# Dealing the row steps of a PEER layer evenly over the late weight units, and making the residual in pieces

## What is computed

```
s1, s2 = q[:, :, 0] @ sub_keys_1.T, q[:, :, 1] @ sub_keys_2.T      # 8 heads, 128 keys each
top 16 of each, top 16 of their sums -> experts (n, 8, 16), gate = softmax(sums)
u   = u_table[experts]                  # 128 rows of 2048 floats for each token
act = gelu(einsum('nhkd,nd->nhk', u, x))
v   = v_table[experts]
out = einsum('nhk,nhkd->nd', gate * act, v)
y   = layer_norm(alpha * x + out)
```

## Time and profile before

| | |
|---|---|
| three runs | 4706.78, 4710.53, 4716.7 us |
| median | 4710.53 us |
| profiled execution | 4703.39 us, its span 4701.6 us |
| mean granted clock of TensorE | 0.965 |
| busy share | PE 92%, DVE 57%, ACT 23%, POOL 55% |
| bytes moved | 1081.84 MB |

### The profile page before, as it was taken

One profiled execution on the slowest core, in us unless ns is written; L12 is line 12 of the kernel. 1 busy time (PEld: TensorE's weight loads), 2 busy tenths in 40 slices (PEclk: granted clock), 3 DMA queues, 4 the chain that ended last, 5 costly groups with the idle time before them and its releaser, 6 DMA issues.

```text
span 4701.6 us, 74886 instructions
## 1 busy us (share of the span) xinstructions
PE 4333.9 (92%) x26508; PEld 4161.2 (89%) x26508; DVE 2686.9 (57%) x4819; ACT 1065.4 (23%) x1872; POOL 2598.3 (55%) x1718
## 2 busy tenths in 40 slices
PE   8999999999989997986877888799999999999996
PEld 8999888888889996985776878799999999999995
DVE  1000233344432315997996777777777777777777
ACT  1000122222221102001221222223332333333223
POOL 4454322222235452442326766688787888888883
PEclk9999999999999999997998988899999999999998
DMA  5222322321243221211448998899999999999995
GB/s 200 96 96 103 113 105 105 125 74 72 82 142 122 95 95 47 69 56 61 171 157 325 381 366 344 329 391 385 390 393 377 385 393 390 390 384 394 392 391 219
DMA packets 265955, 1081.84 MB, mean 230 GB/s; under 512 B 24496, under 2 KB 89136, under 8 KB 181168
## 3 DMA queue, kind: packets, MB, share of 16 engines
q0 software_dynamic: 74736, 544.24, 28.4%
q1 hardware_dynamic: 87840, 388.01, 22.6%
q10 hardware_dynamic: 103328, 148.96, 9.3%
HBM read 1019.65 MB, written 66.85 MB: 231 GB/s over the span
## 4 chain that ended last, share of the span: by engine, by line
PE 49%; issue 21%; DVE 11%; POOL 11%; DMA 6%; ACT 1%; POOLq 0%; DVEq 0%; ACTq 0%
PE banks L464 29%; PE banks L642 6%; PE banks L706 5%; POOL w_lo L329 5%; POOL work L365 4%; DMA work<-in_u_rows,idx 3%; PE banks L533 2%; PE banks L495 1%; PE banks L694 1%; POOL rows_own L365 1%; PE banks L503 1%; DVE work L1390 1%; DVE work L1303 1%; DVE work L1311 1%; DVE mv_hi L1389 1%
## 5 line engine op out<-in xcount | busy, mean ns | idle before, releaser
L329 POOL TENSOR_TENSOR w_lo<-w_raw,w_hi 128x1024 fp32r<-128x1024 f32 x480 | 1159.4, 2416 | 421.5 <-ACT w_hi L1027 418.4
L335 POOL TENSOR_SCALAR w_hi<-w_raw 128x2048 fp32r<-128x2048 f32 x130 | 254.0, 1954 | 1480.2 <-PE banks L464 1268.8
L464 PE MATMUL banks<-mv_hi,w_hi 128*128 128x256 f32 x3648 | 863.9, 318 | 62.7 <-DVE mv_lo L1137 37.2
L464 PE MATMUL banks<-mv_lo,w_hi 128*128 128x256 f32 x3648 | 836.6, 311 | 0.0
L464 PE MATMUL banks<-mv_hi,w_lo 128*128 128x256 f32 x3648 | 835.3, 310 | 0.0
L706 PE MATMUL banks<-mv_hi,w_hi 128*128 128x384 f32 x2048 | 704.4, 344 | 103.8 <-DVE work L1442 79.5
L464 PEld LDWEIGHTS banks<-mv_hi,w_hi 128*128 128x128 f32 x3648 | 652.2, 189 | 127.2 <-issue 102.3
L1027 ACT ACTIVATE w_hi<-w_raw 128x1024 fp32r<-128x1024 f32 x480 | 507.1, 1059 | 1065.3 <-PE banks L706 779.4
L642 PE MATMUL banks<-mv_hi,w_hi 128*128 128x384 f32 x2048 | 701.3, 342 | 44.5 <-POOL w_lo L329 28.6
L706 PE MATMUL banks<-mv_lo,w_hi 128*128 128x384 f32 x2048 | 699.0, 341 | 0.0
L706 PE MATMUL banks<-mv_hi,w_lo 128*128 128x384 f32 x2048 | 697.9, 341 | 0.0
(11 more groups left out here) (159 smaller groups left out, 4821.3 us busy)
## 6 DMA issues: line engine op xcount, KB each, us to landing
w_raw<-in_wstream SPq DMA_DIRECT2D x480, 512.0 KB, 8.1
w_raw<-in_wstream SPq DMA_DIRECT2D x130, 1024.0 KB, 4.8
gate_matrix<-work ACTq DMA_DIRECT2D x12, 2048.0 KB, 6.3
work<-gate_matrix ACTq DMA_DIRECT2D x32, 768.0 KB, 13.1
out_p<-work ACTq DMA_DIRECT2D x34, 320.0 KB, 2.2
work<-out_p ACTq DMA_DIRECT2D x34, 320.0 KB, 3.5
gate_scratch<-work ACTq DMA_DIRECT2D x32, 320.0 KB, 2.2
work<-gate_scratch ACTq DMA_DIRECT2D x16, 640.0 KB, 3.9
```

The costliest lines, as they stand in the source:

```text
L329: pool.tensor_tensor(w_lo[s][:, part], raw[s][:, part], w_hi[s][:, part].bitcast(f32), ALU.subtract) \
L335: pool.tensor_scalar(w_hi[s][:, :], raw[s][:, :], 1.0, 0.0, ALU.mult, ALU.add).then_inc(hi_done, 1)
L464: last = pe.matmul(acc(dst, h), a[s][:, P * k:P * k + P], b[h][:, k, :], start=(k == k_first and n == 0), stop=(k == k_last and n == 2))
```

## The change

The row steps get one list for all 240 late units. `deal()` gives each unit a room (7 for an activation unit, 6 for an output unit, 6, 5, 5.5, 4.5 for those of a mixed trip that also handle the early activations, 2 less in the first four, 0 in the last three) and a cost to each step (2, and 12 for the change of blocks), and deals them in order, so that `STEPS[k]` holds the numbers of unit k's steps. That makes 22, 25, 25 and 25 steps in the mixed trips, 17 or 18 in most groups (18, 18, 18, 17, 18, 18, 18, 17, 17 in groups 8 to 16, 14 in group 17, again 17 or 18 up to group 30, 12 in group 31). Passes no longer begin with a group: A on V begins in group 9, the blocks change in the first unit of group 17, B on V begins in group 24. The end of block B comes two units before the last.

```
+def deal():
+    steps = [[] for _ in ROOM]
...
+    scale = sum(ROOM) / sum(c for _, c in todo)
+    done, slot, room = 0, 0, ROOM[0]
+    for n, c in todo:
+        while room < (done + c / 2) * scale:
+            slot += 1
+            room += ROOM[slot]
+        steps[slot].append(n)
+        done += c
...
-MIXED = [3, 3, 3, 3, 4, 2, 2, 1, 3, 3, 3, 2]
-LATE_STEPS = [[2 * n, 2 * n + 1] for n in range(2 * EG)]
```

GpSimd, VectorE and ScalarE have these units written out instead of looped. The indices are read from `idx_all` directly, without the copy to `idx2` (L354), and the dots go straight to `act_n`, without `dots` and its copy. On GpSimd:

```
+            def position(k):
+                first = (len(STEPS[k]) + 1) // 2
+                for h, part in enumerate((STEPS[k][:first], STEPS[k][first:])):
+                    if k + 2 < len(STEPS):
+                        low(k % 2, k // 2 + 1, h)
+                    for n in part:
+                        if n == STEP_NORM:
+                            norm_store(0)
+                            for z in (0, 2, 3):
+                                gather(STEP_B_U + z)
+                            pool.wait_ge(n_stored, 16)
+                            gather(STEP_B_U + 1)
+                        else:
+                            fetch(n + ROWS)
 
             pool.wait_ge(idx_ready, 1)
-            fetch_idx(0, 0)
+            for n in range(ROWS - 1):
+                gather(n)
+            with pool.Fori((U_PEER + TAIL) // 2 + 1, U_LATE // 2) as i:
+                for s in range(2):
+                    split_next(s, i)
             for s in range(2):
                 for h in range(2):
                     low(s, 0, h)
...
+            for w in range(2):
+                pool.wait_ge(g_stored[w], 16 + 16 * (GBLK // 2))
+            gather(ROWS - 1)
```

```
             dve.wait_ge(picks_taken, 3)
+            dve.wait_ge(hb_stored, 16)
             dve.wait_ge(nat_ready, 2)
+            dve.sem_inc(rows_used, ROWS)
...
-            own.done(dve.tensor_scalar(r_acc, mv_hi[1].bitcast(f32), ALPHA, None, ALU.mult))
-            own.wait()
-            own.done(dve.scalar_tensor_tensor(r_acc, mv_lo[1].bitcast(f32), ALPHA, r_acc, ALU.mult, ALU.add))
...
+            def acc_low(e):
+
+                at = slice(EG * e, EG * e + EG)
+                dve.wait_ge(acc_high, e + 1)
+                own.done(dve.scalar_tensor_tensor(r_acc[:, at, :], mv_lo[1][:, at, :].bitcast(f32), ALPHA, r_acc[:, at, :],
+                                                  ALU.mult, ALU.add))
```

ScalarE serves the two gelus of the weights and the square roots of the norms at the unit where their step lies:

```
+            def serve(k):
+
+                for n in STEPS[k]:
+                    if n == STEP_A_V or n == STEP_B_V:
+                        act.wait_ge(act_n_ready, 1 if n == STEP_A_V else 2)
+                        act_n_gelu_pass()
+                    if n == STEP_NORM:
+                        act.wait_ge(n_var, 1)
+                        act.activation(rstd_n, rstd_n, ACT.Sqrt).then_inc(n_std, 1)
+                if k == STEPS_LAST + 1:
+                    act.wait_ge(n_var, 2)
+                    act.activation(rstd_n, rstd_n, ACT.Sqrt).then_inc(n_std, 1)
```

More of the change, by code:

```diff
@@ L383, in block_b @@
                 pool.dma_start(rows_t[2], hb_s).then_inc(rows_in[2], 16)
[L385 to L400, removed]
@@ L403, in position @@
[L403 to L415, removed]
@@ L417, in late_group, with fetch @@
[L417 to L422 removed]
+            def fetch(n):
+                if n in (STEP_NORM, STEP_NORM + 1):
+                    norm_row(n - STEP_NORM, STEP_NORM)
+                elif n == STEP_NORM + 2:
+                    block_b()
+                elif n in (STEP_END, STEP_END + 1):
+                    norm_row(n - STEP_END, STEP_END)
+                elif n < STEP_END and n != STEP_NORM + 3:
+                    gather(n)
@@ new lines, in steps @@
+            def steps(k, lo=0, hi=None):
+                for n in STEPS[k][lo:hi]:
+                    if n == STEP_NORM:
+                        block_change()
+                        continue
+                    if n == STEP_A_V or n == STEP_B_V:
+                        weights(n // PICKS // 2, n)
+                    gather_step(n)
+                if k == STEPS_LAST + 1 and lo == 0:
+                    norm_stats(1, STEP_END)
+                    norm_out(1, STEP_END)
+            def acc_low(e):
[3 more added lines that the diff above has]
+                                                  ALU.mult, ALU.add))
@@ new lines, in act_units @@
+            def act_units(g, q, k):
+                for e in range(EG):
+                    bank = banks[:, e, 0:N2]
+                    if e == 0:
+                        steps(k)
+                        dve.wait_ge(g4_in, 16 * q + 16)
+                    dve.wait_ge(gelu_done, 4 * g + e + 1)
+                    product(bank, e)
+                    if e < EG - 1:
+                        steps(k + e + 1, 0, 1)
+                    low_part(q, e, 0, bank)
+                    if k < EG:
+                        acc_low(e)
+                    if e < EG - 1:
+                        steps(k + e + 1, 1)
@@ L1567 @@
+            for g in range(2 * EARLY, GROUPS):
+                first, k = U_PEER + 8 * g + EG, U_PEER + 8 * g - U_LATE
+                act_units(g, g, k)
+                for v in range(EG):
+                    steps(k + EG + v, 0, 1 if v else None)
+                    add_out(g, v, first, g == GROUPS - 1, range(2))
+                    if v:
+                        steps(k + EG + v, 1)
+                    add_out(g, v, first, g == GROUPS - 1, range(2, 4))
+            layer_norm(1)
 def kernel(**inputs):
```

313 lines of the change are left out of this document (123 added, 190 removed).

## The result

The changed kernel took 4660.7 us (median of four, 4646.8 to 4672.0) where the kernel before took 4713.1 beside it: a ratio of 0.9893, 95% interval 0.9876 to 0.9911. The direction was right, but the gain is 52 us and not 106: the time lies at the end of the outer range (4555 to 4665) and outside the 4580 to 4635 of the forecast itself.

| piece | before | after | difference | forecast |
|---|---|---|---|---|
| up to the fourth gelu | 2521.2 | 2502.4 | -18.8 | -13 |
| four mixed trips | 546.3 | 448.5 | -97.8 | -115 |
| 23 late groups | 1546.4 | 1611.3 | +64.9 | +22 |
| what follows | 87.7 | 82.9 | -4.8 | 0 |

What follows compares the result with a forecast made beforehand. It took late groups to be bound by TensorE and mixed trips by DMA, with a 421 GB/s ceiling. Terms of -115, +22 and -13 summed to -106 us, giving 4604, between 4580 and 4635, outer range 4555 to 4665.

Steps and rivals of the forecast that it cites:

- What bounds the kernel: Kernel before: late groups bound by TensorE; mixed trips short of DMA by 17 us each, losing 37.
- (1) Trips: Four mixed trips: fewer row steps end the DMA shortage, leaving 107.8 us a trip; -115 us, bounds -135 and -75.
- (2) Groups: Late groups: 17 or 18 steps leave fifteen groups 0.94 us short of DMA; 24 us lost, bounds 0 and 60.
- The shortage sits in the first half: First half of a late group: 10 steps and 4 units need 34.9 us of DMA against 33.3.
- (3) The block change: Block change inside one late unit: 12 us lost where 14.9 were lost before, bounds 5 and 20.
- (4) Head: First four late units: early gathers and a residual in pieces shorten 61.5 us to 48.5; -13, bounds -5 and -18.
- (5) Tail: End of the kernel: second block's statistics delay additions by some 8 us; 0 taken, bounds -4 and +6.
- (6) loops: Written-out loops of VectorE, ScalarE and GpSimd: some 100 more code fetches cost 0, bounds -3 and +10.
- (a): DMA has room above 421 GB/s, so late groups lose nothing more: -147 us, 4563; chance 0.16.
- (b): Mixed trips keep half their loss because gate loads and early activations empty the DMA: 4658; chance 0.20.
- (c): Late groups: row queue crowds out weights, VectorE late at output units, 7.4 us lost in each: 4738; chance 0.07.

Runs made afterwards that it cites:

- Experiment 4: Changed kernel with four buffers for a mixed trip's early activations, all loaded at its start, instead of two used twice: 4623.6 us, ratio 0.9844.
- experiment 2: Changed kernel with row steps dealt as before the change, keeping early gathers, residual in pieces and written-out loops: 4690.1 us, ratio 0.9967.
- experiment 3: Changed kernel without loading the second half of each late weight unit after the first two, old halves being reused: 4620.9 us, ratio 0.9831.
- the split: Edit to the changed kernel: VectorE makes the first two additions of a group's first output unit between its row steps; alone 4689.3 us.
- experiment 1: Changed kernel with the split and nothing else: 4689.3 us, ratio 0.997.
- 5: The changed kernel run again as it is, beside other runs: 4652.8 us, ratio 0.9881.
- 11: Changed kernel with the split, and the gate load issued ahead of the first output unit in groups outside the trips: 4643.7 us, ratio 0.9859.
- 12: Changed kernel with four early activation buffers, late-group room weights 6 and 7, the split, and gate load before the first output unit: 4596.6 us, 0.9764.

## Why the prediction was half right

**What bounds the kernel** held for the trips: short of DMA, and the waits for additions fell from 75 to 32 us (forecast: under 25).

**(1) Trips: -98 instead of -115.** The mechanism was right, the residue too small. 8 us a trip above 99.8 were taken and 12.3 came. The wait for the early activations is 5.2 to 5.7 us of TensorE's time, as assumed, but about 2 us at the second output unit come on top, and both bring time at the lower clock: 0.96 on the mean. Experiment 4 shows the size of the first part: 6.3 us a trip with its share of clock. And 14 of the 98 us are not the dealing's (experiment 2), which the sum gave all to it.

**(2) Groups: +65 with the block change instead of +22.** This is the step that failed, and it failed where it checked VectorE: "a unit with three steps is 3 x 2.28 for the dots, 0.57 and 0.55 for product and low part, 8.0 of 8.32 us". That counts steps at their bare duration. In the changed kernel they follow each other at 3.1 to 3.9 us, most of them waiting for a row, as the prediction itself had read for the trips (about 3.4), so three of them take some 10 us and do not fit into a unit. Where that happens ahead of the first additions, TensorE waits about 2 us. No term of the sum had this cost: it is there with half the weight bytes too, at 342 GB/s, where a group takes 68.8 us, 2.2 above TensorE's own (experiment 3). TensorE's records divide the 80 us that the 23 groups now take above 1530.9 into 52 of idle time (1611.3 less 1559.0 busy) and 28 in which it is busy but slower, with the clock at 0.99 on the mean; 38 had been forecast for both, with the block change.

The other cause is what the full weight bytes do once the place is mended: 71.0 us with the split against 66.7 with the split and half the bytes. In the sum this was a shortage of 0.94 us, from 28.05 MB at 421 GB/s, in 15 groups (by the dealt lists it is 16 of groups 8 to 30). The 421 come from stretches of 17 to 30 us. Whether they hold for a group is not known: the groups that lost nothing carried 412 to 414 GB/s in experiments 1, 5, 11 and 12 and in the changed kernel, and asked for no more. A group of the changed kernel moves 396 x 70.06 us = 27.7 MB on the mean, 416 GB/s over 66.56 us, where the earlier trace rows had shown 390; at 413 it would be 67.1 us, not 70. So the size of the shortage explains little of the loss. What the runs show is lateness: the gate load lands 40 us after its issue, and its late arrival stops VectorE and then TensorE (experiments 1 and 11). How the bytes come to do this is open. "The shortage sits in the first half" was right of the place of the wait.

By the Trainium skill (DMA: Bandwidth & Descriptors, Where 436 GB/s comes from) the ports carry 435 GB/s and the HBM side 358. The runs lie between: 396 to 406 over 23 groups, 412 to 414 over one, so the second figure is no limit here. Neither figure would have given the time.

**(3) The block change** was right in direction: the group with it, from 3578.8 to 3652.3 by its fourth gelus, takes 73.5 us, 7 more than 66.6 and 3.5 more than the mean group, where 12 were taken.

**(4) Head: -18.8 instead of -13.** From the last product of the gate matrix on it is 19.3. The residual's 8.0 us were in the sum; that the first four units have one or two steps instead of three was used only as room for the pieces, and was worth another 5.8.

**(5) Tail, (6) loops.** The end came 4.8 us earlier, just past the bound of 4. Most groups take 66.56 us from written-out code as well, but its 23 groups together took 9.5 us more, with gates that land later (experiment 2); the second instruction queue went from 26 fetches to 48:

```profile
q14 instruction: 48, 0.39, 0.0%
```

**The rivals.** (a), that the late groups lose nothing, is wrong; whether there is headroom above 421 was not seen. (b), trips that keep half their loss, gives 4658 and hits the time, for the wrong reason: it put -74 on the trips and +30 on the groups. A time alone would have confirmed it. (c) had the mechanism of the groups best: VectorE late at the switch to output units, TensorE idle, then slower. It put 4 us of idle time and 3.4 of lower clock on each group; 2.3 and 1.2 came. It was given 0.07.

## What to carry to other kernels

Ahead of an instruction that another engine waits for, count the work at the distance at which it follows itself under load, not at its bare duration. When the loss of a loop is uneven, set its passes beside what each of them was dealt: here that told place from bytes in traces that the averages left open. A rate over a stretch in which an engine waits is no ceiling; look at what the passes that lost nothing carried. When taking away one suspect moves a wait and does not shorten it, take away both before dropping either: here the split alone cost 0.9 us a group, half the bytes alone gave 1.3, and both gave 3.4. Giving each late consumer its own buffer gained 6.3 us a trip (experiment 4).

## What the runs showed of the hardware that was not expected

The DMA share of the profile stood at 1.00 for 390 GB/s and 1.01 for 406, and at 0.94 for 342: it is no measure of what is left.

The three kinds of transfer fared very differently. From the kernel before to experiment 1 the median landing time of a row gather of 1.05 MB went from 8.9 to 9.9 us, that of a weight half of 0.52 MB from 8.2 to 8.3, and that of a gate load of 0.79 MB from 14.7 to 40.0. Load alone does not explain the last: in experiment 2, with the old steps, it was already 29.2. The gate load is the one in small packets, 18.09 MB in 35690, some 500 bytes each, beside 7.3 KB for the gathers (changed kernel, 2951 to 4530: packets, MB, share):

```profile
q0 software_dynamic: 57375, 417.86, 64.7%
...
q10 hardware_dynamic: 35690, 18.09, 4.1%
```

That the packet size is the cause was not tried.
